# Two seams of a seven-product perceptron: fill groups on panels loaded ahead, first products tile by tile, last product joined from PSUM

## The reference

```python
for l in range(2):
    mod = silu(c) @ w_ada[l] + b_ada[l]                 # shifts, scales, gates: 6 x 1024 columns
    p = modulate(rms_norm(x, g_norm1), sh1, sc1) @ w_in # four mixers A, B, C, D and merge gates
    x = x + gt1 * merge(A(p), B(p), C(p), D(p)) @ w_out
    x = x + gt2 * (square(relu(modulate(rms_norm(x, g_norm2), sh2, sc2) @ w_mlp1)) @ w_mlp2)
return rms_norm(x, g_final)
```

## Time and profile before

| | us |
|---|---|
| median of 3 runs | 2458.38 (2457.55 to 2458.41) |
| the profiled execution's own time | 2453.69 |
| its span | 2451.9 |
| PE busy | 2374.6 (97%), PEld 1628.3 |
| DVE, ACT, POOL busy | 970.4, 599.8, 321.1 |
| mean granted PE clock | 0.993 |

### The profile page before, as it was taken

The page is one execution under the profiler, slowest core; times in us unless marked ns, Lnnn a source line. Parts: engine busy times, 40 slices in busy tenths (PEclk is TensorE's granted clock), DMA queues, the critical chain, the costliest instruction groups (busy, mean ns, idle before and its releaser), DMA issues.

```text
span 2451.9 us, 50063 instructions
## 1 busy us (share of the span) xinstructions
PE 2374.6 (97%) x22472; PEld 1628.3 (66%) x22472; DVE 970.4 (40%) x1854; ACT 599.8 (24%) x1246; POOL 321.1 (13%) x247
## 2 busy tenths in 40 slices
PE   6999999999999999999999999999999999999998
PEld 3554564456555555447888887656667767788887
DVE  2552324244545442127773222532454666422101
ACT  3263323132222221001000002342333333211100
POOL 0000000000101000006666551010000110000000
PEclk9999999999999999999999999999999999999999
DMA  7201111233232335223222224212122122245453
GB/s 293 61 18 69 46 59 43 95 97 131 86 128 83 122 115 181 76 77 104 86 86 86 86 86 159 69 65 85 59 87 63 63 62 63 80 146 172 155 152 106
DMA packets 64404, 239.03 MB, mean 97 GB/s; under 512 B 7008, under 2 KB 8048, under 8 KB 63424
## 3 DMA queue, kind: packets, MB, share of 16 engines
q1 hardware_dynamic: 61824, 220.23, 27.8%
q0 software_dynamic: 2368, 15.61, 1.7%
HBM read 234.76 MB, written 1.05 MB: 96 GB/s over the span
## 4 chain that ended last, share of the span: by engine, by line
PE 94%; DVE 2%; issue 1%; ACT 1%; DMA 1%; SPq 1%; POOL 0%; DVEq 0%; ACTq 0%; POOLq 0%
PE psum L420 91%; PE psum L720 2%; DMA arena<-panels 1%; SPq L2504 0%; DVE arena L1169 0%; ACT arena L762 0%; DVE arena L1425 0%; DMA panel_ring<-panels 0%; ACT arena L772 0%; DVE arena L1736 0%; DVE arena L1442 0%; DVE arena L1440 0%; DVE arena L1703 0%; DVE softmax_stats L737 0%; DVE normed L647 0%
## 5 line engine op out<-in xcount | busy, mean ns | idle before, releaser
L420 PE MATMUL psum<-normed,panel_ring 128*128 128x256 f32 (+1 forms) x2880 | 971.2, 484 | 5.4 <-ACT normed L670 1.8
L420 PEld LDWEIGHTS psum<-normed,panel_ring 128*128 128x128 f32 x2880 | 530.8, 190 | 325.9 <-issue 272.9
L420 PE MATMUL psum<-arena 64*64 64x64 f32 (+6 forms) x14040 | 608.9, 252 | 23.3 <-issue 13.7
L420 PEld LDWEIGHTS psum<-arena 64*64 64x64 f32 (+3 forms) x14040 | 433.1, 139 | 247.5 <-issue 181.8
L420 PE MATMUL psum<-arena,panel_ring 128*128 128x256 f32 (+1 forms) x2048 | 550.4, 422 | 2.7 <-issue 2.7
L420 PEld LDWEIGHTS psum<-arena,panel_ring 128*128 128x128 f32 x2048 | 384.4, 190 | 128.5 <-issue 84.7
L737 DVE TENSOR_REDUCE softmax_stats<-psum 128x1 f32<-128x512 f32 (+1 forms) x144 | 83.6, 599 | 171.7 <-PE psum L420 170.4
L762 ACT ACTIVATE arena<-psum,softmax_stats 128x512 f32<-128x512 f32 (+1 forms) x144 | 87.7, 612 | 211.2 <-PE psum L720 102.5
L1169 DVE SCALAR_TENSOR_TENSOR arena<-arena,psum 128x512 f32<-128x512 f32 (+1 forms) x64 | 35.3, 552 | 141.1 <-PE psum L420 127.0
L1154 ACT ACTIVATE arena<-psum 128x512 f32<-128x512 f32 (+1 forms) x64 | 31.3, 490 | 221.2 <-PE psum L420 221.2
L2137 DVE TENSOR_TENSOR arena<-arena,psum 128x512 f32<-128x512 f32 x20 | 13.7, 686 | 172.3 <-PE psum L420 172.3
(11 more groups left out here) (194 smaller groups left out, 1811.8 us busy)
## 6 DMA issues: line engine op xcount, KB each, us to landing
panel_ring<-panels SPq DMA_DIRECT2D x398, 512.0 KB, 3.5
arena<-panels SPq DMA_DIRECT2D x16, 512.0 KB, 14.9
arena<-small_b POOLq DMA_DIRECT2D x2, 2176.0 KB, 9.7
arena<-bias_d POOLq DMA_DIRECT2D x2, 2048.0 KB, 9.8
arena<-x_t SPq DMA_DIRECT2D x2, 1024.0 KB, 7.3
arena<-x_t POOLq DMA_DIRECT2D x1, 2048.0 KB, 14.9
arena<-const_r POOLq DMA_DIRECT2D x2, 800.0 KB, 6.5
arena<-small_c POOLq DMA_DIRECT2D x2, 768.0 KB, 4.6
```

What stands on the lines that cost most here:

```text
L420: return nc.tensor.matmul(out, lhsT, rhs, start=start, stop=stop, skip_group_check=check)
```

## The change

1. **Groups.** (1,9) moves into the fill beside the recurrence, and (0,10) and (0,11) move out of it: 16 groups there instead of 17, and none before the third piece of merge work. (0,10) and (0,11) stand at the first seam. Their eight panels don't go through the ring: SP loads them into the arena's part above the mixers' outputs (free once mixer C's last pair has closed) just before the first perceptron panel in its order, behind a wait for that closing.
2. **First seam.** Three steps of (0,10) stand ahead of the sums, one behind them; four steps of (0,11) (bank 5) behind the spread. m2 of units 0 and 1 go tile by tile: for each k the two units' matmuls, and so m5. The fifth steps of both groups stand between the m2 and the m5 pair on every engine. Then come m6(0), m6(1) (the latter waits for both transposes to be read), and m3, m7, m4, m1 of units 0 and 1. POOL builds in that order. Product 1 accumulates in bank 7.
3. **Second seam.** In the down half DVE applies the residuals of the inner two quarters as soon as it has them, and ACT squares them; product 1 is not added into the quarters in SBUF, but joins as two more residuals that read its PSUM bank. The sum of squares is kept in h[:, 0] and ends at the sixth tile, so PE adds up three times (tiles 0 to 5, 6, 7). A step of group (1,10) (now bank 2) stands ahead of the sums, one behind, two behind the spread (before: none, one, three). The next layer's constants wait for the last of these residuals.
4. **Seam of layer 1.** One step of (1,11) stands ahead of the sums instead of behind them.
5. `mod_ready` becomes one semaphore for each layer.

```diff
@@ Panels, stage_ada.pe, queue of SP
+        def take_ahead(self, l, at, place, slot_in):
+            self.ahead.setdefault(len(self.order), []).append((l, at, place, slot_in))
...
+    seam_at = KT * T + 8 * 7 * (T // 2)
+    seam_panels = carve(seam_at, 8, PANEL).rearrange("p n (k m) -> p n k m", k=KT)
+    is_seam = lambda l, g: l == 0 and g >= 10
...
+                elif is_seam(l, g):
+                    four = [seam_panels[:, 4 * (g - 10) + j] for j in range(4)]
+                    for j, w in enumerate(four):
+                        stream.take_ahead(l, P_ADA + 4 * g + j, w, early_in[g - 10])
+                    e.wait_ge(early_in[g - 10].h, 128)
...
             for n, (l, i) in enumerate(stream.order):
+                for l_ahead, i_ahead, place_ahead, slot_in in stream.ahead.get(n, []):
+                    e_closed = seam_free[0]
+                    eng.wait_ge(e_closed.h, e_closed.at(1))
+                    eng.dma_start(place_ahead, panels[l_ahead, i_ahead].rearrange("p (k m) -> p k m", k=KT)).then_inc(slot_in.h, 16)
@@ stage_mlp7.pe
-            for u in range(2):
-                e.wait_ge(weights.h, weights.at(1 + u))
-                m2(u)
-                yield
-            for u in range(2):
-                e.wait_ge(weights.h, weights.at(3 + u))
-                m5(u)
-                yield
-            for u in range(2):
-                yield from rest(u, 5 + 3 * u)
+            e.wait_ge(weights.h, weights.at(2))
+            for k in range(4):
+                ready.wait(e, k)
+                for u in range(2):
+                    mm(bank(u, 0)[:, half:], wx[:, u, 1, k, :], h[:, k, left], k == 0, k == 3, check=True)
+            yield
+            yield
+            e.wait_ge(weights.h, weights.at(4))
+            for k in range(4):
+                ready.wait(e, 4 + k)
+                for u in range(2):
+                    mm(bank(u, 1)[:, :half], wx[:, u, 2, k, :], h[:, 4 + k, right], k == 0, k == 3, check=True)
+            yield
+            yield
+            e.wait_ge(inputs.h, inputs.at(1))
+            for u in range(2):
+                e.wait_ge(weights.h, weights.at(5 + u))
+                if u == 1:
+                    for freed, n_freed in turned:
+                        e.wait_ge(freed.h, freed.at(n_freed))
+                m6(u, True)
+                yield
...
-            e.wait_ge(added.h, added.at(KT - 2))
-            token_sums(6, acc[:, :n], n, True)
+            e.wait_ge(added.h, added.at(KT - 3))
+            token_sums(6, h[:, 0, tok], n, True)
+            e.wait_ge(squared.h, squared.at(KT - 1))
+            token_sums(6, h[:, KT - 2, tok], n, False)
             e.wait_ge(squared.h, squared.at(KT))
@@ stage_mlp7.act (down half)
-                        e.wait_ge(residual_done.h, residual_done.at(v - NU + 1))
-                        for m in (2 * (v - NU), 2 * (v - NU) + 1):
-                            nc.scalar.activation(h[:, m, tok], x[:, m, tok], ACT.Square).then_inc(squared.h, 1)
+                        mp = v - NU
+                        e.wait_ge(residual_done.h, residual_done.at(2 * mp + 1))
+                        nc.scalar.activation(h[:, 2 * mp, right], x[:, 2 * mp, right], ACT.Square)
+                        nc.scalar.activation(h[:, 2 * mp + 1, left], x[:, 2 * mp + 1, left], ACT.Square)
+                        e.wait_ge(residual_done.h, residual_done.at(2 * mp + 2))
+                        nc.scalar.activation(h[:, 2 * mp, left], x[:, 2 * mp, left], ACT.Square).then_inc(squared.h, 1)
+                        e.wait_ge(emptied.h, emptied.at(v + 1))
+                        nc.scalar.activation(h[:, 2 * mp + 1, right], x[:, 2 * mp + 1, right], ACT.Square).then_inc(squared.h, 1)
@@ stage_mlp7.dve (down half)
-                emptying(NU + mp)
+                v, m1_part = NU + mp, m1_bank(NU + mp)
                 c = cx[:, mp % 2]
+                link(e, inner(v))
+                residual_of(2 * mp, 1, c[:, 1, :])
+                residual_of(2 * mp + 1, 0, c[:, 2, :]).then_inc(residual_done.h, 1)
+                outer_part(v)
                 residual_of(2 * mp, 0, c[:, 0, :])
-                residual_of(2 * mp, 1, c[:, 1, :])
-                residual_of(2 * mp + 1, 0, c[:, 2, :])
-                residual_of(2 * mp + 1, 1, c[:, 3, :]).then_inc(residual_done.h, 1)
+                link(e, residual_of(2 * mp + 1, 1, c[:, 3, :]))
+                e.wait_ge(m1_done.h, m1_done.at(last_of(v) + 1))
+                residual_of(2 * mp, 0, m1_part).then_inc(residual_done.h, 1)
+                residual_of(2 * mp + 1, 1, m1_part).then_inc(emptied.h, 1)
@@ layer
-        modulation = [[a, g] for a, g in [(0, g) for g in range(4, 12)] + [(1, g) for g in range(9)]] if l == 0 else []
+        modulation = [[a, g] for a, g in [(0, g) for g in range(4, 10)] + [(1, g) for g in range(10)]] if l == 0 else []
-                    if modulation and (n or len(others) == 1):
+                    if modulation and n:
```

More of the change, by code:

```diff
@@ L470, in build @@
     c_in, small_in, x_in = sem("c_in"), sem("small_in"), [sem(f"x_in_{n}") for n in range(2)]
-    mod_ready = sem("mod_ready")
+    mod_ready = [sem(f"mod_ready_{l}") for l in range(DEPTH)]
     def stage_start():
@@ L661, in act @@
         def act(e):
[L662 removed]
+            e.wait_ge(mod_ready[l].h, mod_ready[l].at((3 if which else 1)))
             for k in range(KT):
@@ L2428, in layer @@
         place(norm)
-        for stage in behind:
-            place(stage, 4 - stage.placed)
+        for late in behind:
+            place(late, 4 - late.placed)
         norm = stage_modulate(f"norm2_{l}", l, 1, tok, scaled, ready)
@@ L2433, in layer @@
         if l == 0:
-            stage, sums, loadable = stage_mlp7(l, tok, at, ready, closed)
-            place(stage, 14)
+            stage, sums, loadable = stage_mlp7(l, tok, at, ready, closed, [late.parts["turned"] for late in behind])
+            place(stage, 2)
         else:
```

186 lines of the change are left out of this document (112 added, 74 removed).

## The result

The changed kernel takes 2435.19 us (median of 4 runs, 2433.84 to 2436.73) against 2458.39 (4 runs, 2457.55 to 2462.45): 0.9906 of the time, 95% interval 0.9894 to 0.9918, a gain of 23.2 us. The forecast was 7.5 us of gain and a range down to 2445.5, so the kernel is 10 us faster than the range's end.

The account below looks back on a forecast made before the run. PE was taken to bound nearly all of the chain, so only fewer PE instructions or shorter waits help. Terms -2.1 - 1.7 - 3.5 - 0.2 = -7.5 us took the median from 2458.38 to 2450.9 us, range 2445.5 to 2455.5.

Parts of the forecast that it names:

- Fill beside the recurrence: Stretch with the fill groups: one group fewer saves its own PE instructions, -2.1 us, bounds -3.0 and 0.
- rival (f): Beside the recurrence: removing the first group shifts what follows, more waits for DVE L1169; slower, 2466.0 us; chance 0.04.
- First seam: Output projection to unit 2: panel wait gone, 2.7 us rest before the transposes, one low-clock spell; -1.7 us.
- rival (b): Both seams: the clock stays up; first seam -3.4, second -5.0, fill -2.1, giving 2447.9 us; chance 0.20.
- m6(1) with a margin of 0.4 us: First seam: DVE has read both transposes at 1120.9, this product is due at 1121.3, so no wait.
- Panels ahead: Before the first seam: eight early panel loads arrive 29 us before use; PE's 3.6 us panel wait and POOL's go.
- (e): First seam: panels not ahead in effect, the 3.6 us wait stays; total about -3.6, 2454.8 us; chance 0.04.
- Second seam: Layer 0 to layer 1: shorter DVE chain and earlier sums, -3.5 us, first panel's matmuls -0.2; bounds -5.3 and -2.3.
- three signs: Prediction wrong if the fill stretch doesn't shorten, PE waits for a DMA in a seam, or m6(1) or m3(0) waits for DVE.
- Rival (c): First seam gives nothing, transposes' wait and DVE's reading take it back; 5.3 us less, 2453.1 us; chance 0.12.
- POOL beside DVE: Under the output projection: POOL's earlier building would lengthen DVE's adds of squares through the shared port; nothing added.
- S: Theory of the experiments, not the prediction: the gain comes from the first fill group starting later beside the recurrence.

Follow-up runs that it names:

- b16late: Kernel before with the new fill list alone: later start, 16 groups, group (1,8) left out, seams as before; 2443.47 us, 0.9927 of before.
- a_turn_m5: Kernel after with the transposes between m5 and m6 instead of between m2 and m5; 2436.61 us, 0.9915 of before.
- a_ring: Kernel after with the panels of (0,10) and (0,11) on the ring again instead of loaded ahead; 2448.78 us, 0.9967 of before.
- a16pad: Kernel after with five blank steps, empty on every engine, dealt over the recurrence like a group; 2450.44 us, 0.9968 of before.
- a16share17: Kernel after, all instructions kept, five fill steps more dealt over the recurrence; 2448.98 us.
- b17share16: Kernel before, every instruction kept, five fill steps fewer dealt over the recurrence, the rest run behind it; 2450.05 us, 0.9972 of before.

## Why the prediction was wrong

**The failed step** is the term "Fill beside the recurrence: one group fewer, -2.1, bounds -3.0 and 0". It priced the group by its own instructions. In the trace the stretch gave 12.5 us, and alone (b16late, by the medians) 15.5. Split by the two profiles: about 8.0 us less idle time of PE, 1.7 for half the time at 1.2 GHz (3.4 us instead of 6.8, at half rate), 2.1 for the group's instructions, the rest spread. The working had the re-dealing in view, in rival (f), but only as a loss, and only at the wait for DVE L1169. It did not ask whether the deal of before was itself a bad one; the waits put down to "issue", 9.9 us in this stretch, were the sign. The prediction called 6.0 us the largest cause of waits there, which misread that view. And the bounds were drawn around the instruction count, though five empty steps can move this kernel by 15 us.

Point by point:
- *First seam, -1.7 with bounds -3.8 and +0.5*: measured -3.9. The chain was as worked out: sums later by three steps, no wait for POOL, transposes waiting for ACT (2.19 us; 2.7 forecast), unit 2 29.3 us behind the first scaling (29 to 31 forecast), in-place combinations at 1.22 us. What was mis-sized is the clock: I took 3.4 us at 1.2 GHz, and there was none, as in rival (b). That was luck as much as anything: seven of the eleven traces with this seam have a spell. The four in which it lies where the forecast put it, at the rest before the transposes, take 35.9 to 36.1 us, which is 2.2 to 2.5 less than the trace of before. The Trainium skill (TensorE: Matmul & The Clock Gate, "Part 1: The HAM clock gate") holds that the point at which the clock changes varies from run to run. The traces agree as far as they go, being of different kernels with the same seam: of eight with the same rest of 2.19 us before the transposes, the spell began within 1.0 us of the rest's end in four and did not come in the other four.
- *m6(1) with a margin of 0.4 us*: it held, with 0.8 us: DVE had read both transposes at 1107.6, and m6(1), the second half of the record that starts at 1106.64, began near 1108.4. With the transposes moved (a_turn_m5) it turned into a wait of 0.73 us.
- *Panels ahead*: held, and worth more than forecast; (e)'s 3.6 us wait on the ring would have been 3.8 for the second group and 6.4 for POOL (a_ring).
- *Up and down halves, 0*: 360.88 against 360.87.
- *Second seam, -3.5 -0.2*: measured -3.8, with the clock falling behind the sums as taken; in the thirteen traces with this seam -2.2 to -4.7. The last sums end 4.2 us behind the end of the last product (4 to 5.5 forecast).
- *Output projection*: "about 2 us less" was the sign asked for, and 12.5 came. None of the three signs by which the prediction would be wrong came true; they looked only for a gain that is too small.
- *Rival (c)*: its sum, 2.1 + 3.2, doesn't follow from the terms (2.1 + 3.5 + 0.2 = 5.8); nothing hangs on it.
- *POOL beside DVE*: the adds of squares under the output projection (L1842 after) took 0.69 us, but 1.58 where POOL built beside them, as two lines of DVE's timeline below show; it cost nothing, since DVE waits 3.7 to 5.9 us before each tile's residual.

```profile
1077.41 0.69 DVE L1842 TENSOR_TENSOR arena<-arena,normed 128x512 f32<-128x512 f32 x1 [0.69 <-ACT normed L1872]
1084.28 1.58 DVE L1842 TENSOR_TENSOR arena<-arena,normed 128x512 f32<-128x512 f32 x1 [0.70 <-ACT normed L1872]
```

- *Layer 1*: 939.1 against 938.0 us; forecast 0.

**What stays open**: why the deal of 315 steps meets the waits called "issue" and that of 310 meets fewer. They come to 9.0 to 9.9 us in before, a16pad and a16share17, 5.1 in b17share16 and 3.4 in after, and most of them find the whole core idle. The traces point to what they are. One DMA queue (q8) carries instructions in packets of 16 KB: 178 packets in the kernel before, where PE's program has some 45600 instructions (matmuls, weight loads and semaphores), so 256 a packet, if the queue is PE's own. The rest of 3.60 us in a16share17, from 823.15 to 826.75 us, has one of them inside it, from 824.50 to 825.43, as the DMA view of 823.16 to 826.75 us shows:

```profile
q1 hardware_dynamic: 169, 0.59, 40.8%
q8 instruction: 1, 0.02, 1.6%
```

All 119 such rests between 455 and 1105 us, in all eighteen traces, end 1.22 to 1.61 us behind the end of such a packet; of the 244 rests with another cause in the same stretches only ten do. Two packets never start closer than 3.26 us. So PE seems to stand because its next instructions haven't come, where many small matmuls follow each other closely. No run tested it, and why a packet comes late where it does isn't shown. S is not settled by its medians either: the late start gave 4.1 us in the kernel after, though none of it in the recurrence's trace, and in the kernel before its run was disturbed by the ring.

## What to carry to other kernels

Where fill work is dealt over a latency-bound chain by a count, the count is a parameter of its own: price a removed filler by re-dealing, with bounds of both signs, and sweep the count (here -10 to +10 steps moved the time by 20 us) before believing in a change to the fill. Groups whose panels block a ring don't stand back to back in it (8.7 us), and a seam takes more of them only with their panels loaded ahead (13.6 us). Read the waits without a named cause as a sum, too: they may be the largest item that a new order can give back, and hold their ends against the instruction packets of the DMA view. And where the clock may or may not fall in a seam, read the seam from several traces before calling a microsecond of it a gain.

## What the hardware showed

- Idle time of PE that the profile puts down to "issue" varied with the order of the work from 3.4 to 9.9 us in the same 635 to 645 us. Between the kernel after and a16share17, which issue the same instructions, it was 3.4 against 9.3 us, with a single rest of 3.6 us. Each of these rests ended 1.2 to 1.6 us behind a 16 KB instruction packet.
- The time at 1.2 GHz in the recurrence ranged from 0 to 17.1 us between kernels that differ only in a count. In a16share17 it accounts for at most 6.8 of the 13.6 us lost in that stretch ((17.1 - 3.4) at half rate; a spell that falls into a rest costs less); the idle time accounts for another 5.3.
- The same first seam had no time at 1.2 GHz in four traces, a spell of 3.4 us that began around the spread in three, and one that began at the rest of 2.19 us in four. The length of the rest alone did not decide.
- The second seam's way up to the last sums took 4.18 us in all thirteen traces that have the new one, and the sums themselves 1.95 to 3.32 us, by the moment at which the clock fell.
